# Rotation and one gate vector's folds on GpSimd in a three-block transformer kernel

## The reference, cut to what matters

```python
mod = (cond @ ada_w[i] + ada_b[i])[:, None, :]          # cond = silu(c), ada_w[i] is 1024 x 6144
shift1, scale1, gate1, shift2, scale2, gate2 = jnp.split(mod, 6, axis=-1)
h = rmsnorm(x, norm1_g[i]) * (1.0 + scale1) + shift1
qkv = h @ w_qkv                                          # 1024 x 3072
q = jnp.concatenate([apply_rope(q[..., :A_ROT], cos, sin), q[..., A_ROT:]], axis=-1)  # 16 of 64
k = jnp.concatenate([apply_rope(k[..., :A_ROT], cos, sin), k[..., A_ROT:]], axis=-1)
p = jax.nn.softmax(s, axis=-1)                           # two score maps for each of 8 heads
w = (p[:, :, 0] - lam * p[:, :, 1]).astype(v.dtype)
o = rmsnorm(o, subln_g) * (1.0 - lam_init)
x = x + gate1 * (o @ w_o)
```

## Time and profile before

| | |
|---|---|
| median of three executions | 1056.72 us |
| the profiled execution, and its span | 1057.23 us, 1055.5 us |
| TensorE busy | 1001.1 us, 95% of the span |
| VectorE, ScalarE, GpSimd busy | 735.9, 543.0 and 59.3 us |
| moved from HBM | 218 MB, 207 GB/s over the span |
| granted TensorE clock, mean | 0.989 of 2.4 GHz |

### The profile page before, as it was taken

How to read it: one execution, slowest core, us unless ns; L and a number is a source line. 1 busy time by engine, 2 the same in 40 slices (tenths; PEclk the granted TensorE clock), 3 DMA queues, 4 the chain that set the end, 5 groups by cost and what they waited for, 6 DMA issues and landing times.

```text
span 1055.5 us, 12741 instructions
## 1 busy us (share of the span) xinstructions
PE 1001.1 (95%) x4744; PEld 820.3 (78%) x4744; DVE 735.9 (70%) x1030; ACT 543.0 (51%) x882; POOL 59.3 (6%) x100
## 2 busy tenths in 40 slices
PE   3899879999999999999999999999999999999997
PEld 2787567888888877777888887888889878888786
DVE  5989777977768787887765545737654676767753
ACT  3354654644434376665444435665555475555441
POOL 2100021000000410010000001100000010000000
PEclk9999889999999999999999999999999999999999
DMA  9999313998889845248875553856544357665551
GB/s 339 315 370 350 102 61 106 352 342 274 266 299 328 299 160 200 75 125 257 292 227 185 177 197 101 266 170 199 145 134 149 111 183 236 180 182 180 177 179 41
DMA packets 126966, 219.86 MB, mean 208 GB/s; under 512 B 9235, under 2 KB 78088, under 8 KB 126904
## 3 DMA queue, kind: packets, MB, share of 16 engines
q1 hardware_dynamic: 125488, 216.05, 62.3%
q0 software_dynamic: 1088, 2.87, 1.0%
q10 hardware_dynamic: 328, 0.12, 0.0%
HBM read 217.96 MB, written 1.05 MB: 207 GB/s over the span
## 4 chain that ended last, share of the span: by engine, by line
PE 80%; DVE 10%; ACT 4%; DMA 3%; issue 2%; POOL 0%; SPq 0%; DVEq 0%; POOLq 0%; ACTq 0%
PE bank L1815 15%; PE bank L1817 15%; PE bank L1816 15%; PE bank L1830 5%; PE bank L1831 5%; PE bank L1832 5%; DVE w_lo L1100 3%; PE bank L1877 2%; PE bank L1879 2%; PE bank L1878 2%; ACT w_hi L620 1%; DMA raw<-in_a_w_qkv 1%; PE bank L1933 1%; PE bank L1860 1%; PE bank L1909 1%
## 5 line engine op out<-in xcount | busy, mean ns | idle before, releaser
L1100 DVE TENSOR_TENSOR w_lo<-raw,w_hi 128x1024 fp32r<-128x1024 f32 x312 | 378.3, 1223 | 229.2 <-ACT w_hi L620 228.9
L620 ACT ACTIVATE w_hi<-raw 128x1024 fp32r<-128x1024 f32 x312 | 326.3, 1059 | 344.8 <-PE bank L1817 189.0
L1815 PE MATMUL bank<-w_hi,h_hi 128*128 128x512 f32 x768 | 307.4, 400 | 4.6 <-DVE h_lo L1281 2.7
L1817 PE MATMUL bank<-w_hi,h_lo 128*128 128x512 f32 x768 | 300.7, 392 | 0.0
L1816 PE MATMUL bank<-w_lo,h_hi 128*128 128x512 f32 x768 | 300.1, 391 | 0.0
L1815 PEld LDWEIGHTS bank<-w_hi,h_hi 128*128 128x128 f32 x768 | 145.0, 189 | 35.1 <-issue 4.0
L1817 PEld LDWEIGHTS bank<-w_hi,h_lo 128*128 128x128 f32 x768 | 144.8, 189 | 31.1
L1816 PEld LDWEIGHTS bank<-w_lo,h_hi 128*128 128x128 f32 x768 | 145.2, 189 | 29.7 <-issue 1.0
L1830 PE MATMUL bank<-w_hi,u_hi 128*128 128x512 f32 x200 | 78.6, 393 | 0.8 <-ACT av L1047 0.8
L1832 PE MATMUL bank<-w_hi,u_lo 128*128 128x512 f32 x200 | 77.9, 389 | 0.0
L1831 PE MATMUL bank<-w_lo,u_hi 128*128 128x512 f32 x200 | 77.9, 389 | 0.0
(11 more groups left out here) (317 smaller groups left out, 1258.8 us busy)
## 6 DMA issues: line engine op xcount, KB each, us to landing
raw<-in_f_w_in SPq DMA_DIRECT2D x176, 256.0 KB
ada<-in_ada_w SPq DMA_DIRECT2D x86, 512.0 KB, 5.8
raw<-in_w_in SPq DMA_DIRECT2D x46, 512.0 KB
raw<-in_f_w_out SPq DMA_DIRECT2D x44, 512.0 KB
raw<-in_w_up SPq DMA_DIRECT2D x88, 256.0 KB
raw<-in_a_w_qkv SPq DMA_DIRECT2D x24, 512.0 KB
raw<-in_w_down SPq DMA_DIRECT2D x22, 512.0 KB
raw<-in_b_w_qkv SPq DMA_DIRECT2D x12, 512.0 KB
```

Source lines behind the costliest of these rows:

```text
L620: nc.scalar.activation(w_hi[:, m % SPL], raw[:, m % RAW], ACT.Copy).then_inc(hi_done, 1)
L1100: ve.tensor_tensor(w_lo[:, m % SPL], raw[:, m % RAW], w_hi[:, m % SPL].bitcast(F32), ALU.subtract).then_inc(lo_done, 1)
L1815: mm(o, hi, w_hi[:, s, k], start=(u == 0 and k == 0), stop=False)
L1817: last = mm(o, lo, w_hi[:, s, k], start=False, stop=(u == 3 and k == 1))
```

## The change

- The rotation moves from VectorE to GpSimd, in four pieces, one for each chunk of q and k, behind that chunk's copy out of PSUM. TensorE's transposes are spread over steps 13 to 20, one of `qkT`'s pairs a step; at step 13 TensorE also waits until chunk 2 is copied out, whose banks they use.
- The eight folds of `gate1` move from VectorE to GpSimd (`gate_part`), each as two instructions, a product with `cond[:, k]` in place and a sum with `ada_u`. The tiles come into two buffers of their own, `gate_tile`. Parts 0 to 5 stand behind the rotation, 6 and 7 between the first and the second root. SP loads tiles 0 and 1 behind the output projection's first weights, 2 and 3 behind its last two, 4 to 7 behind the first tile of `IN_0`; from tile 2 on each load waits for a sum on GpSimd.
- The folds of vectors 3 and 4 up to 33 are spread over tiles 8 to 26.
- The gate's matmuls and their copies move from the attention to behind the third and fourth tile of the output projection.
- The sums for lambda start four steps earlier and are split in two.

The scores of heads 0 to 2 now stand in a row, and the gate stands between tiles of the output projection. The core of the diff:

```diff
--- before.py
+++ after.py
@@ -55,7 +55,7 @@
 
 def fold_table():
 
-    after = dict(zip(range(16, 34), (6, 8, 9, 11, 12, 14, 15, 16, 18, 19, 20, 22, 23, 24, 26, 27, 28, 29)))
+    after = dict(zip(range(24, 34), (8, 10, 12, 14, 16, 18, 20, 22, 24, 26)))
     after.update({36: 30, 37: 31, 38: 32, 39: 33})
     for a0, q0 in ((40, 39), (48, 52), (56, 65), (64, 78)):
         after.update({a0 + n: q0 + n * 4 // 3 for n in range(8)})
@@ -76,8 +76,7 @@
 SHARED_WITH = {4: 0, 6: 4, 7: 6, 9: 7, 10: 3}
 
 
-QK_STEPS_A = (19, 20, 21, 22)
-QK_ORDER_A = (0, 4, 1, 5, 2, 6, 3, 7)
+QK_STEPS_A = {13 + n: n for n in range(8)}
 
 HEADS_A = ((0, 4), (4, 7), (7, 8))
 
@@ -213,9 +212,10 @@
         row = at_p("row", [P, D], 9216)
         ada_late = at_p("ada_late", [P, D], 8192)
         ada_row = at_p("ada_row", [P, D], 9216)
+        gate_tile = at_p("gate_tile", [P, 2, D], 3072)
         stage_v = at_p("stage_v", [P, 3, P], 10752)
         lam_v = at_p("lam_v", [P, 4, 64], 11136)
-        w_sp = at_p("w_sp", [P, 4, P], 9216)
+        w_sp = at_p("w_sp", [P, 4, P], 5120)
         freq_row = at_p("freq_row", [P, 8], 11392)
         pos_i = at_p("pos_i", [P, T], 11400, I32)
         pos_f = at_p("pos_f", [P, T], 11408)
...
@@ -342,6 +349,12 @@
                 src = w.rearrange("(k p) n -> p k n", p=P)[:, 2 * u:2 * u + 2, cols(c0, turn, per, n)]
                 sp.dma_start(raw[:, m % RAW], src).then_inc(raw_in[m % RAW], 32)
 
+            def load_gate(k):
+
+                if k >= 2:
+                    sp.wait_ge(gate_fold, k - 1)
+                sp.dma_start(gate_tile[:, k % 2], ada_w[0][k * P:(k + 1) * P, 2 * D:3 * D]).then_inc(gate_load[k % 2], 16)
+
             def load_pair(m, w, u, c0, turn=None):
 
                 slot_free(m, turn)
@@ -362,8 +375,10 @@
                 tile, arrived, _ = ada_tile(a)
                 if a in (14, 15):
                     sp.wait_ge(ada_done, a - 14 + 3)
-                if a >= 18:
-                    sp.wait_ge(ada_done, a - ADA_SLOTS + 1)
+                if a in (26, 27):
+                    sp.wait_ge(ada_done, a - 12 + 1)
+                if a >= 28:
+                    sp.wait_ge(ada_done, folded(a - ADA_SLOTS + 1))
                 if a < 16:
                     src = ada_w[0][k * P:(k + 1) * P, 0:2 * D].rearrange("p (v h n) -> p h v n", v=2, h=2)[:, g]
                 else:
@@ -396,10 +411,16 @@
                 load_a(m)
             for j in range(8):
                 load_tall(WO_A + j, a_w_o[0], j)
-
-            for m in range(2):
-                load_pair(IN_0 + m, f_w_in[0], m, 0)
-            for m in range(2, 4):
+                if j == 0:
+                    load_gate(0)
+                    load_gate(1)
+                if j >= 6:
+                    load_gate(j - 4)
+
+            load_pair(IN_0, f_w_in[0], 0, 0)
+            for k in range(4, KD):
+                load_gate(k)
+            for m in range(1, 4):
                 load_pair(IN_0 + m, f_w_in[0], m, 0)
             for m in range(8):
                 load_pair(IN_0 + 4 + m, f_w_in[0], m % 4, (1 + m // 4) * HC)
@@ -553,7 +574,39 @@
             for load in side:
                 load.then_inc(side_in, 16)
 
+            pool.wait_ge(side_in, 16 * SIDE)
+            for c in range(4):
+                pool.wait_ge(evac, c + 1)
+                q = proj[:, :, c * CH:(c + 1) * CH].rearrange("p t (h d) -> p t h d", d=64)[:, :, :, 0:16]
+                tmp = rope_t[:, :, 8 * c:8 * c + 8]
+                spread = lambda tab, n: tab.unsqueeze(2).to_broadcast([P, T, 8, n])
+                for h in range(2):
+                    last = nc.gpsimd.tensor_tensor(tmp[:, :, :, 8 * h:8 * h + 8], q[:, :, :, 8 - 8 * h:16 - 8 * h],
+                                                   spread(rope_a_sb[:, :, 1, 8 * h:8 * h + 8], 8), ALU.mult)
+                last.then_inc(rope_p, 1)
+                pool.wait_ge(rope_p, 2 * c + 1)
+                nc.gpsimd.tensor_tensor(q, q, spread(rope_a_sb[:, :, 0], 16), ALU.mult).then_inc(rope_p, 1)
+                pool.wait_ge(rope_p, 2 * c + 2)
+                nc.gpsimd.tensor_tensor(q, q, tmp, ALU.add).then_inc(rope_c, 1)
+
+            def gate_part(k):
+
+                pool.wait_ge(gate_load[k % 2], 16 * (k // 2 + 1))
+                if k == 0:
+                    pool.wait_ge(bias_in, 16)
+                else:
+                    pool.wait_ge(gate_fold, k)
+                nc.gpsimd.tensor_scalar(gate_tile[:, k % 2], gate_tile[:, k % 2], cond[:, k:k + 1], None,
+                                        ALU.mult).then_inc(gate_mul, 1)
+                pool.wait_ge(gate_mul, k + 1)
+                nc.gpsimd.tensor_tensor(ada_u[:], gate_tile[:, k % 2], ada_u[:], ALU.add).then_inc(gate_fold, 1)
+
+            for k in range(6):
+                gate_part(k)
             for first, end in HEADS_A:
+                if first == 4:
+                    gate_part(6)
+                    gate_part(7)
                 pool.wait_ge(o_sq, end)
                 inv_sqrt(2 * first, 2 * (end - first), P).then_inc(qk_r, 1)
             pool.wait_ge(gate_mm, 2)
@@ -765,11 +818,10 @@
                 last.then_inc(evac, 1)
 
             for m in range(24):
-                if m in QK_STEPS_A:
-                    n = 2 * (m - QK_STEPS_A[0]) + 1
-                    f = QK_ORDER_A[n]
+                if m in QK_STEPS_A and QK_STEPS_A[m] % 2:
+                    n = QK_STEPS_A[m]
                     act.wait_ge(qk_t, n + 1)
-                    nc.scalar.activation(qkT[:, 2 * f:2 * f + 2], bank[4 + n % 4][:].rearrange("p (k s) -> p k s", k=2),
+                    nc.scalar.activation(qkT[:, 2 * n:2 * n + 2], bank[4 + n % 4][:].rearrange("p (k s) -> p k s", k=2),
                                          ACT.Copy).then_inc(qk_a, 1)
                 if m in CHUNK_DONE_A:
                     take_chunk_a(CHUNK_DONE_A[m])
@@ -792,8 +844,6 @@
                                 prob_a[:, i % 2, c, t], bank[2 * (i % 2) + c][:, t * S:(t + 1) * S], ACT.Exp,
                                 bias=stat[:, NMX + n:NMX + n + 1], scale=0.125, accum_out=stat[:, DEN + n:DEN + n + 1])
                     last.then_inc(exp_ok, 1)
-                if i in (1, 2):
-                    gate_half(0, i - 1)
                 if 2 <= i < NH + 2:
                     h = i - 2
                     act.wait_ge(wgt_t, h + 1)
@@ -810,6 +860,8 @@
             operand(1, column=stat[:, MISC + 6:MISC + 7])
             for m in range(WO_A, IN_0 - SKEW):
                 split(m + SPL)
+                if m >= WO_A + 2:
+                    gate_half(0, m - WO_A - 2)
             boundary(0, 0, IN_0, gains, mod[:, 24:32])
 
             def silu(base, f, c, b, turn=None):
...
@@ -1346,9 +1400,15 @@
 
             PI_IN = float(np.nextafter(np.float32(math.pi), np.float32(0)))
             for m in range(16):
+                if m in QK_STEPS_A and QK_STEPS_A[m] % 2 == 0:
+                    n = QK_STEPS_A[m]
+                    v_.wait_ge(qk_t, n + 1)
+                    ve.tensor_copy(qkT[:, 2 * n:2 * n + 2], bank[4 + n % 4][:].rearrange("p (k s) -> p k s", k=2)).then_inc(qk_d, 1)
                 low(QKV_A + SPL + m)
-                if m == 10:
+                if m == 7:
                     minus_lambda()
+                if m == 11:
+                    minus_lambda_end()
 
 
             def rotate(first, heads, table, tmp, need):
@@ -1369,13 +1429,10 @@
                 last.then_inc(rope_ok, 1)
 
             for m in range(16, 24):
-                if m == 16:
-                    rotate(0, 32, rope_a_sb, rope_t, 4)
-                if m in QK_STEPS_A:
-                    n = 2 * (m - QK_STEPS_A[0])
-                    f = QK_ORDER_A[n]
+                if m in QK_STEPS_A and QK_STEPS_A[m] % 2 == 0:
+                    n = QK_STEPS_A[m]
                     v_.wait_ge(qk_t, n + 1)
-                    ve.tensor_copy(qkT[:, 2 * f:2 * f + 2], bank[4 + n % 4][:].rearrange("p (k s) -> p k s", k=2)).then_inc(qk_d, 1)
+                    ve.tensor_copy(qkT[:, 2 * n:2 * n + 2], bank[4 + n % 4][:].rearrange("p (k s) -> p k s", k=2)).then_inc(qk_d, 1)
                 low(QKV_A + SPL + m)
             NH = 8
             def scale_heads(part):
...
@@ -1940,7 +1997,10 @@
             def gate(n, h):
                 g = GATES[n]
                 if h == 0:
-                    pe.wait_ge(ada_done, 8 * (g + 1))
+                    if g == 2:
+                        pe.wait_ge(gate_fold, KD)
+                    else:
+                        pe.wait_ge(ada_done, folded(8 * (g + 1)))
                 if 2 * n + h:
                     pe.wait_ge(gate_ok, 2 * n + h)
                 mm(bank[7][:], ones[:], acc_of(g)[:, h * CH:(h + 1) * CH], start=True, stop=True).then_inc(gate_mm, 1)
@@ -1984,9 +2044,11 @@
 
             for m in range(8, 24):
                 if m in QK_STEPS_A:
-                    pe.wait_ge(rope_ok, 1)
-                    for n in (2 * (m - QK_STEPS_A[0]), 2 * (m - QK_STEPS_A[0]) + 1):
```

(12 more changed lines are left out.)

21 lines of the change are left out of this document (13 added, 8 removed).

## The result

The changed kernel takes 1069.86 us in the median of four executions (1067.38 to 1070.93), the kernel before 1057.20 beside it: a ratio of 1.0114 (95% interval 1.0101 to 1.0126), 12.7 us between the medians. The forecast was 1058.1 and its range ended at 1063.5. The profiled execution took 1067.38 us, its span is 1065.7 us, 10.2 more than before's 1055.5.

The account below looks back on a forecast made before the run. TensorE, busy 95% of the span, bounds the kernel, VectorE pacing the heads from 122.6 to 136.8 us. -8.2 + 1.7 + 4.7 + 3.2 = +1.4 us gave a median of 1058.1, own range 1055.6 to 1060.5, whole range 1052.5 to 1063.5.

Parts of the forecast that it names:

- (a): First projection: moving rotation and eight folds off VectorE ends TensorE's 2.25 us wait and the low clock behind it; -3.9 us.
- (b): Start of the attention: fold 33 stands three weight tiles earlier, so head 0's maximum starts 1.2 us sooner.
- (c): Attention: two gate matmuls leave, removing most of VectorE's 3.32 us idle time; 3.1 us sooner, bounds 0 and 3.3.
- (d): Output projection: two gate matmuls now stand where TensorE waits for nothing, at 0.86 us each; +1.7 us.
- (e): Heads 0 to 3: sums of three GpSimd gate parts hold VectorE's SBUF instructions; +4.7 us, bounds 0 and 10.9.
- (f): Attention's tail: parts 6 and 7 in GpSimd's queue delay the second root and TensorE's transposes; +3.2 us, bounds 0 and 7.
- rival 3: First projection: rotation late or chunk 2 not copied out by step 13, 3.9 us not won; 1062.0 us, chance 0.10.
- (g): SP's queue, second gate's bias row, and fewer loads ahead of weight tiles in the first projection: no effect.
- number 2: Heads 0 to 3 and tail: GpSimd's lock on VectorE costs twice; +6.5 us, 1063.2 us, chance 0.23.
- signs that the prediction named for being right: No TensorE rotation wait, clock 1.00, head 0's maximum near 106.5, VectorE durations 1 to 3 us, 2.4 us sums, later second root.
- those for being wrong: Weights of 0.44 us and attention's end near 141; an end past 150; TensorE idle ahead of step 13, 15, 17 or 19.

Follow-up runs that it names:

- e11: Kernel before with rotation on VectorE, gate1 tiles 0 and 1 on GpSimd ahead of the attention, 2 to 7 folded late by VectorE, gate matmuls late; 1053.03 us, 0.9956.
- e4: Kernel before with only the rotation moved to GpSimd and the transposes spread; folds on VectorE, gate matmuls in the attention; 1059.53 us, 1.0024 of before.
- e3: Changed kernel with the eight gate1 folds back on VectorE and their old loads, gate matmuls still in the output projection; 1059.39 us, 1.0023 of before.
- e1: Changed kernel with gate parts 6 and 7 behind the third root instead of between the first and second; 1060.46 us, 1.0035 of before.
- e9: Kernel before plus a price list of scratch GpSimd operations in the first feed-forward; one execution, 1060.93 us.
- e2: Changed kernel without GpSimd's products with cond, sums alone; 1064.58 us, 1.0069 of before.
- e7: Kernel before plus six scratch sums of 1024 elements on GpSimd from the first scores on; one execution, 1065.32 us.
- e8: Kernel before plus fifteen scratch fills of 1024 elements on GpSimd from the first scores on; one execution, 1058.44 us.
- e6: Changed kernel with the rotation back on VectorE at step 16 and transposes at steps 19 to 22; 1068.95 us, 1.0108 of before.
- e10: Kernel before with VectorE's eight gate1 folds cut to one column, their loads left in place; 1056.84 us, 0.9989 of before.

## Why the prediction was wrong

The forecast was a sum in which terms of both signs nearly cancel, so the sizes decided. Term by term (the measured ones from the tables; they add up, but for rounding, to the +9.6 us at `act_u`; the remaining 0.6 us of the span's 10.2 come later):

| term | forecast | measured | from |
|---|---|---|---|
| (a) first projection | -3.9 | -2.9 | start of the scores |
| (b) + (c) fold 33, gates out of the attention | -4.3 | -3.4 | heads 0-3 of e11, 24.74, against 28.12 |
| (d) gates in the output projection | +1.7 | +1.6 | after against before; 2.0 between e4 and e3 |
| (e) GpSimd beside heads 0 to 3 | +4.7 | +6.4 | heads 0-3, 31.10 against e11's 24.74 |
| (f) parts 6 and 7 between the roots | +3.2 | +8.0 | tail, 18.86 against 10.88 |
| sum | +1.4 | +9.7 | |

The forecast missed by 8.3 us of this sum: 4.8 in (f), 1.7 in (e), 1.0 in (a) and 0.9 in (b) and (c), less 0.1 in (d). The split between (b) + (c) and (e) takes e11's attention as the changed kernel's without GpSimd, which is argued and not shown; their sum, +3.0, is measured directly.

**(f) is the term that failed.** The mechanism was right, and e1 shows it: the queue order costs 7.5 us. The size was wrong, mostly by one price. The product with a scalar was put at 1.1 us, from a one-input select of 512 elements that took 0.63; it takes 2.85. Two of them are 3.5 us more. The select was the wrong row to go by: a product with a constant on as many elements takes 1.49 (e9). And the waits of GpSimd's four instructions for VectorE were put at 1.5 us together; beside VectorE's folds and scaling the sum was stretched to 4.23 us and the product to 3.62, 2.7 more than by themselves. So two parts took 13.4 us (138.88 to 152.25) where 8.7 were forecast, 7.2 and the 1.5, and the second root ended at 154.0 where the forecast had 147.6 and those 1.5. The 3.5 and 1.2 us are nearly the whole of the term's error, and the measured 8.0 lies above its stated bound of 7.

**(e) was 1.7 us short.** The forecast had three sums that hold the weights or start under a maximum, and the product as harmless. Four sums came, since part 2 waited for its tile to 105.55 and a part took 5.4 us instead of 3.6. They fell on VectorE's small operation behind each maximum (1.80, 0.64, 2.27 and once more 2.28 us instead of 0.17), and the products took 0.68 from the weights twice. That adds up to 6.3 us for the sums, 1.6 each where the forecast had 1.75, and 1.4 for the products; 6.4 of the 7.7 reached the first root. So the number of sums and the products were wrong here, and not the price of a sum. e2 and e7 show the sums as the cause; e8 and the one-input product, which holds VectorE only in its first 0.9 us, show that GpSimd's being busy is not.

**(a) had the right sign by a wrong reason,** and that it came near was luck. It gave the gain to the rotation's move. e4 shows that this move costs 2.5 us to the scores (111.48 against 109.00; 1.0 of it is TensorE's wait, 3.21 us instead of 2.25, and the rest is open): that is rival 3, with its mechanism and not its price, and the prediction gave it 0.10 because it counted the slack of the last chunk and not that of chunk 2 at step 13. e6 shows that the gain comes with the folds and loads that left the stretch, and e10 that it is not the folds' time. In the changed kernel TensorE still waited 0.76 us at step 13. (The -2.9 us is the best of four profiles with this first projection; the other three give -1.8 to -2.2.) GpSimd's rotation itself took 4.4 to 6.1 us a chunk beside VectorE's work, where the forecast had 2.4, and came in time by its wide cover. The sentence in (g) that TensorE waits for none of those loads, "nothing", was the error: by e6 and e10 VectorE's rotation stood behind weight tiles that came late, and its lateness was what TensorE waited for.

(b) and (c) gave 0.9 us less than forecast together; (c) is 2.0 by e4 and e3, not 3.1: with the gate gone, TensorE's wait for ScalarE's exponentials grew from 3.18 us in e4 to 4.23 in e3. (d) came as forecast: its row was one of the same instruction in a busy stream. Of the rivals, number 2 (the lock costs twice, 1063.2) named the place, and (e) and (f) together, 14.4 us, are near its 13; it kept the gains at 8.2, of which 6.3 came.

Of the signs that the prediction named for being right, most were there (a clock of 1.00 to the end of the first projection, sums of 2.34 us, durations of 1 to 3 us on `stat` and `prob_a`, a late second root), and they say nothing of the sizes. Of those for being wrong, two came: an end of the attention past 150 us, and idle time of TensorE ahead of step 13.

## What to carry to other kernels

A price for an operation that the trace doesn't have should keep the far end of its bounds until it is measured, above all where it stands in a queue ahead of something on the path: here the path was named rightly, and one price put at 1.1 us instead of 2.85 made 3.5 us of the miss. Before work is moved to an idle engine, ask what is next in that engine's queue and what it shares with the engine that it relieves; where VectorE set the pace, 14.6 us of GpSimd's two-input work cost 6.3 us of the attention's time. And a wait for a computation can be a late load one step further back: take the computation away and leave its loads, as e10 did, and see whether the wait goes.

## What the runs showed of the hardware

- GpSimd in float32 over 1024 elements for each partition: sum of two tensors 2.34 us, product with a broadcast column by the two-input form 1.89, product with a column by the one-input form 2.85 (with a constant 3.09 at the least, beside VectorE's work), fill 0.95. The one-input form is the slowest of these.
- What GpSimd does decides how it holds VectorE. Instructions with two tensor inputs hold VectorE's two-input SBUF instructions, even one of 128x2, to their end (2.30 instead of 0.22 us), and its small operation with a constant as well (2.27 instead of 0.17); fills don't (0.88 stays 0.88), and the one-input product does it in part: the weights that ran inside one took 1.56 us and were done before it was (116.80 + 1.56 = 118.36, the product ends at 119.42). Worked out from the rows, that hold ends 0.9 us behind the product's start (116.57, 122.01 and 138.88 in the changed kernel), and VectorE's subtraction of 1024 elements that starts 1.03 us behind another's (106.58 and 105.55) takes its 1.22 us. An exclusive hold for a whole instruction, as the Trainium skill has it (SBUF — State Buffer, "Who interferes with whom"), fits the sums and the two-input product; the one-input product it does not fit, and why is open.
- It works both ways: beside VectorE's fold of 1024 elements and its scaling a sum on GpSimd took 4.23 us instead of 2.34, and beside the rest of another fold a one-input product took 3.62 instead of 2.85.
